# The rotary steps of the next head, moved from the end of an attention step to a place inside it

## The reference, cut to what matters

```
s = einsum('bhqmd,bhkmd->bhmqk', q, k) * scale      # two score maps, m = 0 and 1
p = softmax(s, axis=-1)
a = p[:, :, 0] - lam * p[:, :, 1]
o = einsum('bhqk,bhkd->bhqd', a, v)
```

```
concatenate([x1 * cos - x2 * sin, x2 * cos + x1 * sin])
```

## Time and profile before

| | |
|---|---|
| median of three runs | 2940.73 us |
| profiled execution, its own time | 2940.5 us |
| its span | 2938.6 us |
| TensorE (PE) busy | 2877.4 us, 98% |
| DVE busy | 1330.6 us, 45% |
| ScalarE (ACT) busy | 1076.5 us, 37% |
| POOL busy | 614.0 us, 21% |
| chain that ended last | PE 89%, DVE 5% |

### The profile page before, as it was taken

The page is one execution under the profiler, slowest core; times in us unless marked ns, Lnnn a source line. Parts: engine busy times, 40 slices in busy tenths (PEclk is TensorE's granted clock), DMA queues, the critical chain, the costliest instruction groups (busy, mean ns, idle before and its releaser), DMA issues.

```text
span 2938.6 us, 44082 instructions
## 1 busy us (share of the span) xinstructions
PE 2877.4 (98%) x18396; PEld 2756.4 (94%) x18396; DVE 1330.6 (45%) x2291; ACT 1076.5 (37%) x1947; POOL 614.0 (21%) x312
## 2 busy tenths in 40 slices
PE   6999999999999999999999999999999999999998
PEld 5999999999999999999999999999999989899997
DVE  4343443123557575446344434421146567554543
ACT  4333333221444544422343333323133444443231
POOL 0221221122221212122431221211221121211242
PEclk9999999999999999999999999999999999999999
DMA  5332224102111102254421121220211111215532
GB/s 224 102 110 82 102 90 137 67 15 78 42 47 47 48 32 94 80 203 141 133 79 65 66 82 39 94 83 22 70 41 45 44 48 47 78 51 183 165 110 94
DMA packets 84278, 248.55 MB, mean 85 GB/s; under 512 B 9201, under 2 KB 30193, under 8 KB 83057
## 3 DMA queue, kind: packets, MB, share of 16 engines
q1 hardware_dynamic: 84080, 245.74, 24.5%
HBM read 191.71 MB, written 54.00 MB: 84 GB/s over the span
## 4 chain that ended last, share of the span: by engine, by line
PE 89%; DVE 5%; ACT 2%; DMA 2%; issue 1%; SPq 1%; DVEq 0%; POOL 0%; POOLq 0%; ACTq 0%
PE ps L730 44%; PE ps L713 18%; PE ps L823 6%; PE ps L769 6%; PE ps L900 3%; PE ps L1041 3%; PE ps L1032 2%; PE ps L961 2%; PE ps L888 2%; PE ps L943 1%; DVE e L1839 1%; DVE stat L1822 1%; ACT e L1435 1%; DMA wmod<-w_mod 1%; DVE aTl L1846 1%
## 5 line engine op out<-in xcount | busy, mean ns | idle before, releaser
L730 PE MATMUL ps<-hhi,whi 128*128 128x384 f32 x2640 | 916.3, 347 | 5.7 <-DVE obuf L1854 3.3
L730 PE MATMUL ps<-hhi,wlo 128*128 128x384 f32 x2640 | 886.3, 336 | 0.0
L730 PE MATMUL ps<-hlo,whi 128*128 128x384 f32 x2640 | 884.1, 335 | 0.0
L1956 POOL TENSOR_TENSOR wlo<-wraw,whi 128x1024 fp32r<-128x1024 f32 (+1 forms) x188 | 415.8, 2212 | 2063.6 <-ACT whi L1127 2063.5
L730 PEld LDWEIGHTS ps<-hhi,whi 128*128 128x128 f32 x2640 | 500.0, 189 | 24.1 <-issue 7.3
L730 PEld LDWEIGHTS ps<-hlo,whi 128*128 128x128 f32 x2640 | 497.1, 188 | 0.9
L730 PEld LDWEIGHTS ps<-hhi,wlo 128*128 128x128 f32 x2640 | 495.9, 188 | 0.0
L1127 ACT ACTIVATE whi<-wraw 128x1024 fp32r<-128x1024 f32 (+1 forms) x188 | 174.5, 928 | 229.9 <-PE ps L713 209.3
L1444 ACT ACTIVATE aTh<-ps 128x512 fp32r<-128x512 f32 (+1 forms) x200 | 96.5, 482 | 278.4 <-PE ps L1032 278.4
L1691 DVE TENSOR_TENSOR ptl<-ps,pth 128x512 fp32r<-128x512 f32 (+1 forms) x144 | 82.1, 611 | 246.8 <-ACT pth L1301 246.6
L1822 DVE TENSOR_REDUCE stat<-ps 128x1 f32<-128x1152 f32 x144 | 176.5, 1231 | 16.9 <-PE ps L769 16.0
(11 more groups left out here) (199 smaller groups left out, 4835.8 us busy)
## 6 DMA issues: line engine op xcount, KB each, us to landing
wraw<-w_in SPq DMA_DIRECT2D x128, 512.0 KB, 4.2
gates_dram<-gst SPq DMA_DIRECT2D x48, 576.0 KB, 3.0
gth<-gates_dram SPq DMA_DIRECT2D x48, 576.0 KB, 4.9
mraw<-w_mod SPq DMA_DIRECT2D x32, 512.0 KB, 3.8
wraw<-w_branch SPq DMA_DIRECT2D x48, 256.0 KB, 2.8
bias<-rpb SPq DMA_DIRECT2D x8, 1280.0 KB, 6.0
outs_dram<-obuf SPq DMA_DIRECT2D x16, 576.0 KB, 3.9
oraw<-outs_dram SPq DMA_DIRECT2D x16, 576.0 KB, 3.8
```

Source lines behind the costliest of these rows:

```text
L730: x = mm(ps[:, bank, 0:CH], a[:, s % 2, k, :], b[:, k, n * CH:(n + 1) * CH], start=(k == 0 and a is whi and b is hhi), stop=(k == KT - 1 a ...
L1956: g_.tensor_tensor(lo[:, 0:kt, :], wraw[:, n % 2, 0:kt, :], hi[:, 0:kt, :].bitcast(F32), ALU.subtract).then_inc(S.w_lo, 1)
```

## The change

The loop over the parts that a step's entry in `turns` names becomes a function, `turn(t)`. It was called at the end of a step, behind `out_pair`; it is called behind `lows(t, 2)` and ahead of `scaled_e2(t + 1)`. Parts, table and instructions are the same.

```diff
+                    def turn(t):
+
+                        for r, part in turns.get(t, "").split():
+                            dve.wait_ge(*unit_evac((r, l, "df", h + 1), NC - 1))
+                            rotated(qraw if r == "q" else kraw, int(part))
+
...
                             lows(t, 2)
+                            turn(t)
                             scaled_e2(t + 1)
                             combined(t + 1)
...
                         if t % 2 or t == LT:
                             out_pair(t // 2)
-                        for r, part in turns.get(t, "").split():
-                            dve.wait_ge(*unit_evac((r, l, "df", h + 1), NC - 1))
-                            rotated(qraw if r == "q" else kraw, int(part))
```

## The result

| | before | after |
|---|---|---|
| median of six runs each | 2940.94 us (2940.19 to 2942.31) | 2950.89 us (2949.41 to 2953.68) |
| ratio | | 1.0035, 95% interval 1.0024 to 1.0046 |
| profiled execution, span | 2940.5, 2938.6 us | 2949.4, 2947.4 us |
| DVE busy | 1330.6 us | 1325.2 us |
| granted clock, mean | 0.996 | 0.994 |

The change made the kernel 9.95 us slower. The forecast was 6 us slower, 2946.7 us with a range up to 2949.0, and the measured time lies above the range. The profiled execution after is the fastest of its six runs.

What follows compares the result with a forecast made beforehand. TensorE, busy 2877.4 of 2938.6 us, was taken as the bound. Heads 1 and 2 at 1.04 us each, four times 4.2, plus head 0's 1.8 gave +6.0 us, 2946.7 us; own range 2945.5 to 2948.2, widened to 2941.0 to 2949.0.

Steps and rivals of the forecast that it cites:

- What comes, the double part of step 4: q3 and k0 ahead of step 4's scaling: PE starts 0.89 us late in head 0, 2.80 in heads 1 and 2.
- the old wait: PE's wait for `aTl` at `probs_t(5, 1)`, heads 1 and 2: claimed to go whole, saving 1.09 us.
- Forecast -1.09 + 0.06: Heads 1 and 2: PE's stall at `probs_t(7, 1)` goes, 1.09 us; a single part's reciprocal comes 0.06 us late.
- step 7: k3 ahead of the 128-wide scaling, which waits for POOL's `ql`: costs 0.3 us a head in heads 1 and 2.
- The first rival: Step 4: the scaling does not wait for POOL, only `combined` does: +0.9 us, 2941.6 us; chance 0.16.
- The second rival: At `combined(5)` of heads 1 and 2 neither scaling nor `combined` waits: -2.9 us, 2937.8 us; chance 0.07.
- The third rival: Steps 2 and 6: POOL takes the port before `combined`, 1.8 us at up to ten places, up to +18 us; chance 0.08.
- waited for a projection: Rival: moved parts wait for a projection ACT has not evacuated and hold up `combined`, a few us slower; chance 0.03.
- the rotary's products: Sign: all 48 rotary parts inside the loops take 1.2 to 1.3 us, so L1803's median is 1225 ns.

Runs made afterwards that it cites:

- the second trace: The changed kernel run once more without any further change, to get a second trace: 2952.88 us in one run.

## Why the prediction was wrong

The direction was right and so was nearly every step of the mechanism. The step that failed is the term "What comes, the double part of step 4", with its 2.80 us for heads 1 and 2: it ended with PE's start. It should have gone on to what TensorE's clock does behind such a wait.

Head 1 of layer 0, by how far PE runs behind the trace of before:

- At `probs_t(4, 0)` 938.68 - 936.00 = 2.68 us; 1.67 of that comes from the prologue, 0.96 from head 0. Forecast for head 0: 0.89.
- At `probs_t(5, 0)` 952.89 - 947.52 = 5.37, so +2.69. Forecast +2.80: the scaling ended 0.62 us behind POOL where I had taken 0.88 - 0.15 = 0.73, and PE's start came 0.14 behind `combined` as taken.
- At `probs_t(5, 1)` 958.03 - 952.19 = 5.84, so +0.47. Forecast -1.09: the old wait went as forecast, and 1.56 us of low clock came, which the forecast does not have at all. 4 x 1.56 = 6.2 us.
- At `probs_t(7, 1)` 979.14 - 974.40 = 4.74, so -1.10 for both steps together. Forecast -1.09 + 0.06.
- At step 8's unit 986.88 - 982.08 = 4.80, so +0.06. Forecast +0.3. The mechanism was there, the 128-wide scaling waited for `ql` and took 2.47 us:

```profile
982.21 1.23 DVE L1807 TENSOR_TENSOR kraw<-xc,xr 128x1024 f32<-128x1024 f32 x1
983.36 0.16 DVE L1830 RECIPROCAL stat<-stat 128x2 f32<-128x2 f32 x1
983.59 2.47 DVE L1832 TENSOR_SCALAR e<-e,stat,neglam 128x128 f32<-128x128 f32 x1
986.14 0.35 DVE L1839 SCALAR_TENSOR_TENSOR e<-e,stat,e 128x128 f32<-128x128 f32 x1
```

  but it replaced a wait for `obuf` of the same 0.41 us almost whole.

Added up, the head costs 0.05 + 2.69 + 0.47 - 1.10 + 0.06 = 2.2 us instead of 1.04. Four heads give 8.7 and head 0 1.9: 10.6 us in all. So the low clock, 6.2 us, is more than the whole miss. Without it the change would have cost 4.4 us against the 6.0 forecast, most of the difference from step 7 (0.06 us a head for 0.3). The two errors lie in opposite directions, and the smaller one made the forecast look nearer than its mechanism was.

The two profiled executions differ by 8.9 us and not by 10.6, since other places differ as well: +1.7 us in the first 50 us, -1.6 at the start of layer 1, where the clock fell in the trace before and not in the trace after, and -0.9 where a wait of PE for a weight chunk (up to 1254.18 before) is gone. The remaining -0.9 is spread over the rest. The first two also differ between the two traces of the changed kernel. That the medians' 9.95 us come out near 10.6 is therefore in part luck; what shows the cause is the set of kernels above.

The first rival (the scaling does not wait) fell: its maximum is 2.68 us. The rule of the Trainium skill that I had weighed (SBUF — State Buffer, "Who interferes with whom") holds for the scaling as well, and the kernel in which POOL waits shows it from the other side. The second rival (a gain) needed `wlo` later than the scaling; with POOL made to wait it came true, 2936.9 against 2937.8 forecast for it. The third rival did not happen at steps 2 and 6, where `combined` stayed 0.12 us or more ahead of `wlo` and kept its 1.42 us, but it shows its price at step 4 with the shuffle alone. Nothing waited for a projection. As forecast, the rotary's products run at their free 1.23 us inside the loops (L1803's median went from 2920 to 1226 ns).

The range failed with the term. Its upper end of 2949 came from 0.1 to 0.2 us a place and left no room for a price that goes with the length of a wait. The changed kernel's runs also spread over 4.3 us where before spreads over 2.1 in as many; the second trace, with its longer fall at 952, shows a source of that.

## What to carry to other kernels

Price a new wait of the engine that bounds the kernel together with what it runs like afterwards: look for an old wait of that length and read the granted clock behind it, in more than one trace, since one of ours fell in only five of ten. A filler belongs into an idle gap only up to the gap's length plus the slack behind it, and the slack differs by step: two parts in step 4 cost some 20 us against one, three parts in step 1 nothing that the time shows. Where DVE and POOL follow each other by one or two tenths of a microsecond, a small delay of DVE can turn their order round.

## What the runs showed of the hardware

- TensorE's clock fell to 1.2 GHz behind idle times of 2.35, 2.54 and 2.95 us (15 places of 15 in the attention steps of five traces), and did not there behind 0.63, 0.75, 1.28 and 1.65 to 1.66 us. What lies between 1.66 and 2.35 us was not tried. The wait of 2.44 us at the start of layer 1 has a fall behind it in five of ten traces, and the 1.62 us between the layers in one of ten, so length does not decide alone.
- A `tensor_scalar` of 1152 or 128 columns with one SBUF source waited for POOL like an instruction with two: 2.68 us for 0.88, and 2.47 for 0.35. It ended 0.62 us behind POOL at 1152 columns and 0.09 at 128, each time 0.26 less than its free time.
- The order of the recorded starts does not quite tell who waits: `combined` with a start 0.12 us or more ahead of `wlo` kept its 1.42 us in all traces, with 0.03 to 0.04 us ahead it waited, four times of four.
